# The norm behind the output projection of a two-layer block: ScalarE squares every tile, GpSimd adds, and two feature sums stand inside the last tile's products

## The reference, cut to what matters

```python
def second_block(x, mem, positions, g_pre_mix, w_in, ...):
    for l in range(DEPTH):                       # DEPTH = 2
        h = _rmsnorm(x, g_pre_mix[l])
        z = h @ w_in[l]
...
        y = jnp.concatenate([_rmsnorm(y_f, ...), _rmsnorm(y_a, ...), _rmsnorm(y_m, ...)], axis=-1) @ w_out[l]
        x = x + _rmsnorm(y, g_post_mix[l])

        h = _rmsnorm(x, g_pre_ffn[l])
        gate, up = jnp.split(h @ w_ffn_in[l], 2, axis=-1)
        f = (jax.nn.silu(gate) * up) @ w_ffn_out[l]
        x = x + _rmsnorm(f, g_post_ffn[l])
```

## Time and profile before

| | |
|---|---|
| three runs, us | 1974.85, 1973.76, 1972.62 |
| median | 1973.76 us |
| profiled execution, span on the core | 1969.7 us |
| PE busy | 1833.7 us (93%) |
| VectorE, ScalarE, GpSimd busy | 1240.9, 850.8, 318.0 us |

### The profile page before, as it was taken

One profiled execution on the slowest core, in us unless ns is written; L12 is line 12 of the kernel. 1 busy time (PEld: TensorE's weight loads), 2 busy tenths in 40 slices (PEclk: granted clock), 3 DMA queues, 4 the chain that ended last, 5 costly groups with the idle time before them and its releaser, 6 DMA issues. The chain is left out here.

```text
span 1969.7 us, 42687 instructions
## 1 busy us (share of the span) xinstructions
PE 1833.7 (93%) x18256; PEld 1604.7 (81%) x18256; DVE 1240.9 (63%) x2163; ACT 850.8 (43%) x1561; POOL 318.0 (16%) x361
## 2 busy tenths in 40 slices
PE   7999877968999999999999799999889999889997
PEld 5787436858688888888878699999689999789997
DVE  4574886676656424533766778745868656767753
ACT  4321566354423212222437345534744355554432
POOL 0201205335140000013002121012040012030001
PEclk9999988979999999999999999999989999999998
DMA  9752940020522323232420366555145465226552
GB/s 329 206 181 80 306 150 3 2 66 2 172 86 87 106 86 107 86 98 74 150 64 1 100 194 180 190 179 167 44 150 183 140 195 190 87 87 209 177 162 95
DMA packets 248982, 254.68 MB, mean 129 GB/s; under 512 B 6914, under 2 KB 247187, under 8 KB 248691
## 3 DMA queue, kind: packets, MB, share of 16 engines
q1 hardware_dynamic: 239214, 242.86, 38.7%
q10 hardware_dynamic: 8740, 8.51, 1.3%
q0 software_dynamic: 864, 0.98, 0.3%
HBM read 251.29 MB, written 1.05 MB: 128 GB/s over the span
## 5 line engine op out<-in xcount | busy, mean ns | idle before, releaser
L578 DVE TENSOR_TENSOR RING_rounded<-RING,SC_rounded 128x1024 fp32r<-128x1024 f32 (+2 forms) x390 | 460.0, 1222 | 234.8 <-ACT SC_rounded L571 234.4
L598 PE MATMUL bank<-OT_rounded,SC_rounded 128*128 128x256 f32 (+1 forms) x1808 | 575.8, 318 | 15.6 <-DVE HT_rounded L1173 6.8
L600 PE MATMUL bank<-OT_rounded,RING_rounded 128*128 128x256 f32 (+1 forms) x1808 | 571.7, 316 | 0.0
L599 PE MATMUL bank<-HT_rounded,SC_rounded 128*128 128x256 f32 (+1 forms) x1808 | 570.7, 316 | 0.0
L571 ACT ACTIVATE SC_rounded<-RING 128x1024 fp32r<-128x1024 f32 (+2 forms) x390 | 374.0, 1010 | 358.9 <-DMA RING<-in_l_mlp_w 182.6
L598 PEld LDWEIGHTS bank<-OT_rounded,SC_rounded 128*128 128x128 f32 x1808 | 344.4, 191 | 44.8 <-issue 8.8
L600 PEld LDWEIGHTS bank<-OT_rounded,RING_rounded 128*128 128x128 f32 x1808 | 343.0, 190 | 23.8
L599 PEld LDWEIGHTS bank<-HT_rounded,SC_rounded 128*128 128x128 f32 x1808 | 343.0, 190 | 23.3
L598 PE MATMUL bank<-PT_rounded,SC_rounded 128*128 128x256 f32 (+1 forms) x896 | 277.2, 309 | 5.5 <-DVE RING_rounded L578 5.5
L600 PE MATMUL bank<-PT_rounded,RING_rounded 128*128 128x256 f32 (+1 forms) x896 | 277.2, 309 | 0.0
L599 PE MATMUL bank<-PT_rounded,SC_rounded 128*128 128x256 f32 (+1 forms) x896 | 276.8, 309 | 0.0
(11 more groups left out here) (574 smaller groups left out, 2777.0 us busy)
## 6 DMA issues: line engine op xcount, KB each, us to landing
RING<-in_l_mlp_w SPq DMA_DIRECT2D x64, 1024.0 KB, 5.5
RING<-in_w_ffn_in SPq DMA_DIRECT2D x44, 1024.0 KB, 5.1
RING<-in_l_mod_w SPq DMA_DIRECT2D x32, 1024.0 KB, 6.6
RING<-in_l_w_in SPq DMA_DIRECT2D x25, 1024.0 KB, 6.0
RING<-in_w_ffn_out SPq DMA_DIRECT2D x16, 768.0 KB, 4.9
RING<-in_w_in SPq DMA_DIRECT2D x10, 1024.0 KB, 5.5
RING<-in_w_ffn_out SPq DMA_DIRECT2D x16, 640.0 KB, 4.6
PT<-in_l_mod_w SPq DMA_DIRECT2D x8, 1024.0 KB, 10.1
```

Source lines behind the costliest of these rows:

```text
L578: net.nc.vector.tensor_tensor(low, whole, net.high4(s, m)[:, 0:self.w.kts[s], :].bitcast(F32), ALU.subtract).then_inc(self.split_ready, 1)
L598: net.nc.tensor.matmul(bank[:, tokens], high, x_high, start=start, stop=False)
L599: net.nc.tensor.matmul(bank[:, tokens], high, x_low, start=False, stop=False)
L600: return net.nc.tensor.matmul(bank[:, tokens], low, x_high, start=False, stop=stop)
```

## The change

ScalarE squares all eight tiles ahead of their copies (`square_tile`), the first six into six further buffers (`y_squares`, with a semaphore `y_squared`), and GpSimd only adds them (`add_tile_squares`, five adds). `sum_first` can be called in parts. Its first two products stand inside the last half of `out`, behind the rows 4 and 6, the third behind it. `renew` has a new order wherever there is a y, thus in all four `mixed` and `fed`: a tile's scale, the low part of the tile before, then the add. In `fed` the rest stays as it is.

```diff
--- before.py
+++ after.py
@@ -599,13 +599,15 @@
         net.nc.tensor.matmul(bank[:, tokens], high, x_low, start=False, stop=False)
         return net.nc.tensor.matmul(bank[:, tokens], low, x_high, start=False, stop=stop)
 
-    def half(self, pe, q, m, tokens, wait=None):
+    def half(self, pe, q, m, tokens, wait=None, behind={}):
 
         self.ready(pe, q, m)
         for kt in range(self.w.kts[q % SLOTS]):
             if wait:
                 pe.wait_ge(wait[0], wait[1] + kt)
             last = self.passes(q, m, kt, tokens)
+            if kt in behind:
+                behind[kt]()
         last.then_inc(self.used, 1)
 
 
@@ -1112,12 +1114,13 @@
         self.net, self.y, self.y_gains, self.gains = net, y, y_gains, gains
         self.x = [net.XT[:, t, 0:LAT] for t in range(KT)]
         (self.sums_ready, self.last_square, self.summed, self.root_ready, self.renewed, self.high_ready,
-         self.split_ready, self.x_squared) = (
+         self.split_ready, self.x_squared, self.y_squared) = (
             st.sem(f"{name}_{what}") for what in ("sums_ready", "last_square", "summed", "root_ready", "renewed",
-                                                  "high_ready", "split_ready", "x_squared"))
+                                                  "high_ready", "split_ready", "x_squared", "y_squared"))
         self.sums, self.sums_2 = net.G2[:, 0:LAT], net.G2[:, LAT:2 * LAT]
         self.last_squares = [self.sums_2, net.WDG[:, :, :].rearrange("p t m -> p (t m)")]
         self.squares = [net.PT[:, 24 + t, 0:LAT] for t in range(KT)]
+        self.y_squares = [net.PT[:, 24 + t, LAT:TOK] for t in range(KT - 2)]
         self.scratch = net.LORA[:, 1, 0:LAT]
         self.r1, self.r2 = net.SC[:, 8192:8448], net.SC[:, 8448:8704]
 
@@ -1136,17 +1139,37 @@
             else:
                 step.then_inc(self.sums_ready, 1)
 
+    def square_tile(self, act, t, of):
+
+        if t < KT - 2:
+            act.activation(self.y_squares[t], of, ACT.Square).then_inc(self.y_squared, 1)
+        else:
+            self.square_last(act, t - KT + 2, of)
+
+    def add_tile_squares(self, pool, link):
+
+        for t in range(1, KT - 2):
+            pool.wait_ge(self.y_squared, t + 1)
+            step = pool.tensor_tensor(self.sums, self.y_squares[0] if t == 1 else self.sums, self.y_squares[t], ALU.add)
+            if t < KT - 3:
+                link(step)
+            else:
+                step.then_inc(self.sums_ready, 1)
+
     def square_last(self, act, n, of):
         act.activation(self.last_squares[n], of, ACT.Square).then_inc(self.last_square, 1)
 
-    def sum_first(self, pe):
-        nc, ones, total = self.net.nc, self.net.const(C_ONES), self.net.ps[6][:, 0:LAT]
-        pe.wait_ge(self.sums_ready, 1)
-        nc.tensor.matmul(total, ones, self.sums, start=True, stop=False)
-        pe.wait_ge(self.last_square, 1)
-        nc.tensor.matmul(total, ones, self.last_squares[0], start=False, stop=False)
-        pe.wait_ge(self.last_square, 2)
-        nc.tensor.matmul(total, ones, self.last_squares[1], start=False, stop=True).then_inc(self.summed, 1)
+    def sum_first(self, pe, some=range(3)):
+        ones, total = self.net.const(C_ONES), self.net.ps[6][:, 0:LAT]
+        for n in some:
+            if n == 0:
+                pe.wait_ge(self.sums_ready, 1)
+            else:
+                pe.wait_ge(self.last_square, n)
+            step = self.net.nc.tensor.matmul(total, ones, self.last_squares[n - 1] if n else self.sums, start=(n == 0),
+                                             stop=(n == 2))
+        if 2 in some:
+            step.then_inc(self.summed, 1)
 
     def root_first(self, act, link):
         act.wait_ge(self.summed, 1)
@@ -1174,15 +1197,17 @@
                                         self.net.OR[:, t, 0:LAT].bitcast(F32), ALU.mult,
                                         ALU.subtract).then_inc(self.split_ready, 1)
 
-        scaled = {0: scale(0)}
         for t in range(KT):
-            if t + 1 < KT:
-                scaled[t + 1] = scale(t + 1)
             if y:
-                link.until(scaled[t])
-                vector.tensor_tensor(x[t], x[t], y[t], ALU.add).then_inc(self.renewed, 1)
+                scaled = scale(t)
+            else:
+                for n in (0, 1) if t == 0 else (t + 1,) if t + 1 < KT else ():
+                    scale(n)
             if self.gains and t:
                 low(t - 1)
+            if y:
+                link.until(scaled)
+                vector.tensor_tensor(x[t], x[t], y[t], ALU.add).then_inc(self.renewed, 1)
             if t in between:
                 between[t]()
         if self.gains:
@@ -2030,7 +2055,7 @@
             add_pair(pool, 6, 7)
             pool.wait_ge(mixers.squared, 4)
             add_pair(pool, 2, 3)
-            mixed.add_first_squares(pool, link, out)
+            mixed.add_tile_squares(pool, link)
             mixed.add_second_squares(pool, link)
             fed.add_first_squares(pool, link, down)
             if not last:
@@ -2058,10 +2083,10 @@
             sum_tile(2, 5, False, True)
             pe.wait_ge(group_root, 2)
             rows_side_by_side(pe, out, 0, group_split, order)
-            for q in range(2, out.total):
-                for m in range(2):
-                    out.half(pe, q, m, lats)
-            mixed.sum_first(pe)
+            for q, m in ((2, 0), (2, 1), (3, 0)):
+                out.half(pe, q, m, lats)
+            out.half(pe, 3, 1, lats, behind={4: lambda: mixed.sum_first(pe, (0,)), 6: lambda: mixed.sum_first(pe, (1,))})
+            mixed.sum_first(pe, (2,))
             rows_side_by_side(pe, gates, 0, mixed.split_ready)
             for q in range(2, gates.total):
                 for m in range(2):
@@ -2122,8 +2147,7 @@
                 for m in range(2):
                     if part is out:
                         act.wait_ge(out.used, 2 * q + m + 1)
-                        if out.tile(q, m) >= KT - 2:
-                            mixed.square_last(act, m, out.bank(q, m)[:, lats])
+                        mixed.square_tile(act, out.tile(q, m), out.bank(q, m)[:, lats])
                         act.activation(PT[:, 2 * q + m, lats], out.bank(q, m)[:, lats], ACT.Copy).then_inc(out.taken, 1)
                     elif part is gates and q % 2 == 0:
                         whole = hidden.whole[:, q + m, :]
```

## The result

Six runs of the changed kernel have a median of 1983.59 us (1978.06 to 1986.22), six of the kernel before beside them 1973.19 (1967.90 to 1975.28). The ratio is 1.0052, with a 95% interval of 1.0035 to 1.0068: 7 to 13 us slower. I had forecast 6 us more (1980.0, range to 1983.0); the way was right and the size too small.

What follows compares the result with a forecast made beforehand. TensorE, busy 93% of the span, was taken as the bound, so its stalls count. Terms 0.0, +0.9, +2.4 and +0.9 gave +4.2, the clock +2; added to the 1973.76 us median, 1980.0, range 1974.5 to 1983.0.

Steps and rivals of the forecast that it cites:

- What sets the point: Second sum behind the projection: GpSimd's adds, begun after the last low part, set its start; PE's earlier arrival is worth nothing.
- The turn: Renewal on VectorE and ScalarE: add, high part and low part in a chain take 1.40 us a tile; row 7 2.3 later.
- Layer 0's log to sum: Layer 0, from the logarithm behind the projection to PE's second sum: 2.3 us longer through the later last low part.
- layer 1's 2.3 - 0.4: Layer 1, logarithm to second sum: last low part 2.3 us later, less 0.4 us free between GpSimd's end and PE's sum.
- the feed-forward's +2.4: Renewal behind layer 0's feed-forward: last low part at 1663.8, not 1661.40; PE already waits for GpSimd's adds, so 2.4 us later.
- the end's +0.9: Kernel's last renewal: each add waits for its scale, a tile takes 0.86 us, not 0.73; PE ends 0.9 us later.
- Part 1: First sum behind the projection: ScalarE's squares and two sums inside the last tile bring the logarithm 2.3 and 1.0 us earlier.
- The clock: TensorE's granted clock falls behind the new stalls ahead of the second sums: +2 us, 1.5 for the longest, 0.5 for two others.
- The third fall: Clock fall behind the 1.9 us stall after layer 0's feed-forward, sharing 0.5 us with layer 1's; all three falls: chance 0.10.

Runs made afterwards that it cites:

- e4_no_gate: The changed kernel, but GpSimd begins the second squares' adds without waiting for the eighth low part: 1977.99 us, ratio 1.0023 to the kernel before.
- e8_gap: e6_squares with 7 products of constants in PE's wait for the first renewed row: 1967.92 us, ratio 0.9988 to the kernel before.
- e2_order: The kernel before with the renewal's new order alone: 1985.90 us, ratio 1.0057 to the kernel before.
- e3_last_old: The changed kernel with the old order in the last renewal only: in one execution 16.67 us from the last logarithm to the end, not 17.64.
- e5_fill: The changed kernel with products of constants on PE while it waits for GpSimd ahead of the second sum: 1977.69 us, ratio 1.0029 to the kernel before.
- e6_squares: The changed kernel with the renewal's old order and all three first sums behind the last tile again: 1967.68 us, ratio 0.9988 to the kernel before.

## Why the prediction fell short

- **What sets the point.** Right. The second sum is held by GpSimd, which is held by the last low part; e4_no_gate takes that hold away and the wait with it, e8_gap shows that PE's own speed doesn't matter there, and e2_order that the new order alone carries the loss.
- **The turn** was given as 1.40 us and the last low part as 12.4 behind the first scale; measured 1.40 and 12.44. Layer 0's log to sum +2.3 (measured 2.27), layer 1's 2.3 - 0.4 (1.90), the feed-forward's +2.4 (2.50), the end's +0.9 (0.9 to the last transposes, 1.15 to the end; e3_last_old puts 1.0 on the order). So the mechanism and this price were right.
- **Part 1 was over-rated.** I had the logarithms 2.3 and 1.0 us earlier; it was 1.6 and 0.6. I took a sum among the products at 0.43 us from a row at the kernel's end, where three sums follow one another; inside the tile each cost 0.57. GpSimd came 0.33 and 0.27 too late, where I had 0.1 and 0.25, and the last square and the sum left took 1.2 from the last product on, where I had 1.1. That is 1.1 of the 3.7 us that were missing.
- **The clock was the term that failed.** I gave 2.0 us, it was 4.3 by the marks (2.50 and 1.79) and 4.65 by e5_fill, over both stalls; this is 2.3 of the missing 3.7. I took part of the slow stretch to be hidden in the stall itself; but the clock fell only in the last 1.3 us of layer 0's stall, and in layer 1 it was at 1.00 up to the sum (1782 to 1784); then it stayed low for 20 products in layer 0 and 11 in layer 1, at 0.213 us from one to the next and not 0.118, with the sum itself slow. I had also given the layer 1 stall of 2.3 us no more than 0.5, together with the third. The third fall, behind the feed-forward, didn't come: PE met its delay in pieces of 1.0, 0.9 (in two) and 0.4.
- The rest of the difference between 9.9 and the forecast 6.2 is the end's 0.25 and 0.1 behind the feed-forward. The medians differ by 10.4, and 1983.59 lies 0.6 us over my range. Its upper end held the falls of the clock, but not those together with a first part worth a third less.

## What to carry to other kernels

When a stall goes, find out which engine is next late at the following meeting point: here the second sum in layer 0 was already set by GpSimd's end to 0.1 us (in layer 1 to 0.4), so that PE's time won ahead of it was worth nothing and every delay of GpSimd's start counted in full. An order that lets one engine fetch the other's result at once (add, high part, low part, next add) makes each turn a sum over both engines; a tile of lead between them costs 0.3 us on the first row and here saves 2.3 on the last. And a short sum was cheaper behind a tile (by 1.2 to 1.3 us a layer), beside the work of another engine that it has to wait for anyway, than among the tile's products.

## What was not expected of the hardware

The same wait of 3.39 us for the first row was followed by a clock of 0.50 before and by 1.00 in e6_squares in layer 0, and by 0.58 there in layer 1:

```profile
1455.10:1459.10 4.00, 3.92 (x33) 3.92 (x34) 4.00 (x11) 3.67 (x9) 0.00 (x0) 1.00 0.00 0
1760.00:1764.00 4.00, 4.00 (x24) 4.00 (x23) 4.00 (x9) 3.05 (x7) 0.00 (x0) 0.58 0.00 0
```

Nor does a wait's length alone order the cases. Waits of 2.31 us (layer 1 of the changed kernel) and 2.15 us (layer 0 of e2_order) were followed by a low clock, and those of 2.09 (e8_gap) were not; but behind the wait of only 1.78 us in the kernel before the clock was low on the mean of the sums:

```profile
1446.50:1449.00 2.50, 2.46 (x6) 1.50 (x6) 0.00 (x0) 0.00 (x0) 0.00 (x0) 0.61 1.06 369
```

So in this kernel the price of such a stall, 1 to 2.7 us, comes or doesn't; what decides it is open, and an estimate has to carry both.

The start of the projection's tile 0 in layer 0 lies between 1430.4 and 1438.2 us in the ten profiles, though all ten kernels are the same ahead of it. From there on the stretch from the feed-forward's sum to layer 1's tile 0 agrees to about 0.1 us (66.27 to 66.39 in the table), and the long ones from a sum to the next logarithm, where the clock stays at full, to about 0.5 (179.35 to 179.83, 177.56 to 178.03). Single runs of one kernel spread by 7 to 14 us; how much of that lies ahead of the mark isn't shown, as each kernel has one profile, but the mark itself moves by 8. So the marks can tell apart what the medians of 12 runs can't, down to about 0.5 us a stretch.

Products of constants that nobody reads kept the clock at full (e5_fill, e8_gap). In e5_fill that was worth 4.65 us; in layer 1 of e8_gap the 1.45 us that PE won by it were waited off at the second sum.
